# Two norm weights kept in the row ring of an expert-gathering decoder layer: twelve gather slots instead of fourteen

## The reference, cut to what matters

```
h  = x + mix
hn = rmsnorm(h, norm_ffn_w)
qry = hn @ w_q                      # 8 heads, two halves of 128
sv, si = top_k(scores, 16)          # per half
fv, fi = top_k(sums of pairs, 16)   # 16 experts per head, 128 picks per token
ue, ve = u[eidx], v[eidx]           # rows of 1024 floats, 4 KB each
act = gelu(einsum('thkd,td->thk', ue, hn))
y  = h + einsum('thk,thkd->td', gate * act, ve)
out = rmsnorm(y, norm_final_w)
```

## Time and profile before

| | us |
|---|---|
| median of three runs | 3558.62 |
| profiled execution, its time | 3555.45 |
| its span, first to last instruction | 3553.6 |
| PE busy | 2983.7 (84%) |
| POOL busy | 2434.8 (69%) |
| DVE busy | 2123.3 (60%) |
| ACT busy | 1522.3 (43%) |
| mean rate of the DMAs | 344 GB/s |

### The profile page before, as it was taken

One profiled execution on the slowest core, in us unless ns is written; L12 is line 12 of the kernel. 1 busy time (PEld: TensorE's weight loads), 2 busy tenths in 40 slices (PEclk: granted clock), 3 DMA queues, 4 the chain that ended last, 5 costly groups with the idle time before them and its releaser, 6 DMA issues.

```text
span 3553.6 us, 30435 instructions
## 1 busy us (share of the span) xinstructions
PE 2983.7 (84%) x8213; PEld 1385.9 (39%) x8213; DVE 2123.3 (60%) x4852; ACT 1522.3 (43%) x4094; POOL 2434.8 (69%) x2228
## 2 busy tenths in 40 slices
PE   6989699987898689878897889689968896589966
PEld 4844246443343244324432344234423442244221
DVE  2221655584658665866577657766676668454674
ACT  2021165334643474346533653365336633353333
POOL 1211276677777777777777777777777777576886
PEclk9999899999999999989998999899999999898999
DMA  5722499999999999999999999999999999898988
GB/s 189 264 83 70 151 405 354 358 341 385 385 388 375 369 394 379 388 370 402 370 395 362 405 372 380 370 407 374 392 359 407 381 388 359 317 358 308 347 315 346
DMA packets 346900, 1222.30 MB, mean 344 GB/s; under 512 B 39931, under 2 KB 51644, under 8 KB 345564
## 3 DMA queue, kind: packets, MB, share of 16 engines
q0 software_dynamic: 314272, 1140.57, 84.1%
q1 hardware_dynamic: 23596, 66.42, 5.1%
q10 hardware_dynamic: 8864, 13.37, 1.1%
HBM read 1195.56 MB, written 25.66 MB: 344 GB/s over the span
## 4 chain that ended last, share of the span: by engine, by line
PE 45%; POOL 21%; DMA 16%; DVE 8%; issue 7%; ACT 2%; SPq 0%; POOLq 0%; ACTq 0%; DVEq 0%
PE ps L1063 23%; DMA rows<-in_peer_v,idx 14%; POOL rows L452 11%; POOL rows L462 11%; PE ps L949 7%; PE ps L819 4%; PE ps L935 3%; PE ps L787 2%; DVE rows L1462 2%; PE ps L837 2%; DMA rows<-in_peer_u,idx 1%; DVE r L1353 1%; DVE r L1346 1%; PE ps L806 1%; DVE r L1347 1%
## 5 line engine op out<-in xcount | busy, mean ns | idle before, releaser
L1063 PE MATMUL ps<-rows,diag 128*128 128x512 f32 (+1 forms) x4224 | 2075.3, 624 | 468.9 <-DMA rows<-in_peer_v,idx 290.9
L1462 DVE CUSTOM_DVE_ANT_0 rows<-rows,hn_u 128x1024 f32<-128x1024 f32 x1056 | 1272.5, 1222 | 799.3 <-DMA rows<-in_peer_u,idx 794.8
L462 POOL DMA_INDIRECT rows<-in_peer_v,idx x1056 | 1200.5, 1137 | 429.7 <-issue 245.5
L1063 PEld LDWEIGHTS ps<-rows,diag 128*128 128x128 f32 (+1 forms) x4224 | 773.1, 195 | 1619.9 <-issue 1235.0
L452 POOL DMA_INDIRECT rows<-in_peer_u,idx x1056 | 1164.6, 1103 | 341.1 <-issue 321.7
L722 ACT ACTIVATE act_g<-act_g 128x1 f32<-128x1 f32 x1056 | 212.0, 201 | 1253.2 <-DVE act_g L1462 1245.9
L728 ACT ACTIVATE diag<-ident,act_g 128x128 f32<-128x128 f32 x1024 | 411.2, 402 | 344.1 <-PE ps L1063 317.1
L724 ACT ACTIVATE act_g<-act_g,gate 128x1 f32<-128x1 f32 x1056 | 311.0, 295 | 34.3
L949 PE MATMUL ps<-w_sc,r 128*128 128x512 f32 (+1 forms) x576 | 280.2, 594 | 0.0
L482 POOL DMA_DIRECT2D rows<-in_w_in x22 | 11.9, 539 | 228.9 <-PE ps L819 218.0
L722 ACT ACT_TABLE_LOAD x124 | 159.1, 1283 | 2.2
(11 more groups left out here) (270 smaller groups left out, 2114.1 us busy)
## 6 DMA issues: line engine op xcount, KB each, us to landing
rows<-in_w_in POOLq DMA_DIRECT2D x36, 512.0 KB, 3.9
rows<-in_peer_u,idx POOLq DMA_INDIRECT x1056, 6.6
rows<-in_peer_v,idx POOLq DMA_INDIRECT x1056, 6.6
r<-proj SPq DMA_DIRECT2D x8, 1344.0 KB, 10.5
rows<-in_w_in ACTq DMA_DIRECT2D x20, 512.0 KB, 6.6
w_sc<-in_w_q_t SPq DMA_DIRECT2D x8, 1024.0 KB, 7.4
proj<-rows POOLq DMA_DIRECT2D x22, 256.0 KB, 3.9
w_o<-in_w_in POOLq DMA_DIRECT2D x10, 512.0 KB, 6.6
```

The lines of the kernel that those rows point to most:

```text
L462: nc.gpsimd.indirect_dma_start(ring[:, slot, :], None, a["peer_v"], bass.IndirectOffsetOnAxis(ap=idx[g % 2][:, k:k + 1], axis=0), engine_s ...
L1063: last = nc.tensor.matmul(Y[j][0:m, :], diag[:, n % DIAGS, 0:m], ring[:, slot, 512 * j:512 * (j + 1)], start=(k == 0), stop=(k == steps_of ...
L1462: V.tensor_tensor_reduce(ring[:, slot, :], ring[:, slot, :], hn_u[:, :], 1.0, 0.0, ALU.mult, ALU.add, act_g[:, k:k + 1]).then_inc(S["dots" ...
```

## The change

Slots 12 and 13 leave the ring. They are named `w_ffn` and `w_fin`, and hold the two norm weights from the setup to the end. SP loads each once, in `load_front(0)`, after a wait for the last use of `keys` (`m_kept`). The loads per tile are gone, with SP's waits for `hn_taken` (except for the sampled tokens' own) and for `topk_done` ahead of them. The norm reads `w_ffn` instead of `hn`. The ring has 5 slots for `u` and 3 for `v` during tile 0, and 7 and 5 from tile 1 on. Slot 5 passes from `u` to `v`.

```diff
-U_EARLY, U_LATE = (0, 1, 2, 3, 4, 5), (8, 9)
-V_EARLY, V_LATE = (6, 7, 12, 13), (10, 11)
+U_EARLY, U_LATE = (0, 1, 2, 3, 4), (8, 9)
+V_EARLY, V_LATE = (5, 6, 7), (10, 11)
@@
-        w_fin = r2[:, D:2 * D]
+        w_ffn, w_fin = ring[:, 12, :], ring[:, 13, :]
@@ load_front(f)
                 if not is_sample(f):
                     sp.dma_start(pj, proj[f, :, 0:CHUNKS - 1, :]).then_inc(S["proj_in"], 16)
-                    if f:
-                        sp.wait_ge(S["hn_taken"], f)
-                    sp.dma_start(hn[:, :], a["norm_ffn"]).then_inc(S["w_ffn_in"], 16)
+                    if f == 0:
+                        sp.wait_ge(S["m_kept"], 2 * PH)
+                        sp.dma_start(w_ffn, a["norm_ffn"]).then_inc(S["w_ffn_in"], 16)
+                        sp.dma_start(w_fin, a["norm_final"]).then_inc(S["w_fin_in"], 16)
                     if f:
                         sp.wait_ge(S["kv_shifted"], f + 1)
                     sp.dma_start(k_t[:, 1, :], proj[f, :, CHUNKS - 1, :]).then_inc(S["proj_in"], 16)
@@ sample_caches(f)
                 sp.wait_ge(S["pv"], 2 * f + 2)
-                sp.dma_start(hn[0:NS, :], a["norm_ffn"][0:NS, :]).then_inc(S["w_ffn_in"], 16)
@@ SP, end of a period
-                    if f is not None:
-                        sp.wait_ge(S["topk_done"], f + 1)
-                        sp.dma_start(w_fin, a["norm_final"]).then_inc(S["w_fin_in"], 16)
@@ DVE, front(k, f), q == 87
-                    dve.wait_ge(S["w_ffn_in"], 16 * f + 16)
+                    dve.wait_ge(S["w_ffn_in"], 16)
-                    V.scalar_tensor_tensor(hn[0:n, :], hx[0:n, :], rstd[0:n, :], hn[0:n, :], ALU.mult, ALU.mult)\
+                    V.scalar_tensor_tensor(hn[0:n, :], hx[0:n, :], rstd[0:n, :], w_ffn[0:n, :], ALU.mult, ALU.mult)\
@@ DVE, finish(k, w), k == 4
-                    dve.wait_ge(S["w_fin_in"], 16 * min(w + 1, TILES))
+                    dve.wait_ge(S["w_fin_in"], 16)
```

## The result

The changed kernel takes 3602.14 us (median of 6 runs, 3595.63 to 3609.92) against 3565.03 us of the kernel before, run beside it (median of 6). The ratio is 1.0107 with a 95% interval of 1.0084 to 1.0130: 1.1% slower, or 37 us between the medians. The forecast was 3596 us and +37 us. That the sum came out does not say that its terms did, and three of them did not (tile 0's size, the setup and tile 7).

What follows compares the result with a forecast made beforehand. Six tiles were taken as bound by POOL's instruction stream and DVE's effect on it, not slots or bytes. Terms -1 + 2 + 22 + 8 + 6 = +37 us gave 3596 us, 1.0% slower, range 3553 to 3645.

Steps and rivals of the forecast that it cites:

- three signs that would have refuted it: Tiles 1 to 6 each 2 us shorter or more, tile 0 within 5 us of 414, or u gathers waiting for dots.
- The loads: Whole kernel: 7.5 MB less weight traffic, covered by POOL's stream, gives back 1 us, at most 18.
- The setup: Before the gathers: k_t issues near 170.0 us, lands 5.6 to 10.6 us later, PE stalls: +2 us.
- Tile 0: First tile with three v slots instead of four: longer rounds per pick, +22 us in all, from 3 to 44.
- Its first part: Tile 0's first 27 or so picks: three-slot rounds exceed POOL's 2.56 us pace, +8 us, from 3 to 12.
- its last: Tile 0 from 740 to 834 us: three-slot rounds and dots held back by DVE's top-k, +9 us, 0 to 24.
- the middle: Tile 0, 510 to 740 us: free while PE is full, except at three pauses of the added work, +5 us.
- Tiles 1 to 6: With five v slots POOL runs out one pick earlier at the last top-k steps: +8 us, 0 to 15.
- Tile 7: POOL is one pick less ahead when each of two clusters of PE stalls ends: +6 us, 0 to 15.
- The first rival: Bytes count after all: 18 us come back and the shorter ring costs little, 3543 us; chance 0.11.
- The second (all hidden): Landings shrink with the ring, lost picks are caught up; little but the setup's 2 us stays, 3561 us; chance 0.10.
- The third (lateness adds up, 3646 us): Landings don't shrink and tile 0, tiles 1 to 6, tile 7 and setup all cost more: +87 us; chance 0.19.

Runs made afterwards that it cites:

- second pair: Kernel before and changed kernel, both run and profiled again on one chip of 3565 us: ratios 0.9994 and 1.0099, profiled at 3586.97 and 3580.70 us.
- first pair: The original profiled executions of the kernel before and the changed kernel: 3555.45 us before, a span of 3599.1 us after.
- the even splits: Changed kernel with 4 u and 4 v slots in tile 0, 6 and 6 after, without or with the weights' loads moved later: 0.9987 each.
- e1_slots_only: Kernel before with the ring cut to 5 and 3 slots in tile 0, 7 and 5 after, all loads kept: 1.0046.
- e7_tile0_three: Kernel before with three v slots instead of four in tile 0 alone, full ring afterwards, loads kept: 1.0082.

## Why the prediction was right, and where it was not

The mechanism was right for tile 0: its loss is `v`'s slots, and neither bytes nor the sum of slots. The sum was +37 us, the medians give +37 and +34. That it fits so closely is partly luck: tile 0 was taken 5 to 13 us too low, the setup and tile 7 some 7 to 11 us too high, and 8 us for tiles 1 to 6 can be neither confirmed nor refused. Of the signs named, the landings near 6 us came, and the thirty first `v` gathers are 3.1 us apart, though only 14 of them show a wait for PE and not nearly each. Tile 0 (449 us for 436), tile 4 (373 for 360 to 368), tile 7 (435 for 445) and the first transposes (174.56 for 176 or later) were off. None of the three signs that would have refuted it came in this profile. In the second pair tiles 1 to 6 did fall by 5 us each, but there the longest execution of the one stands beside the shortest of the other. Term by term:

- **The loads** (-1, ends 0 and -18). Right as far as it was tested: the loads alone gave 3 us beside the full ring, with 0.5% excluded, on a chip of 3735 us. Beside the short ring they may be worth more: on the chip of 3565 us POOL's waits in tiles 1 to 6 are 13 us less without them (17.8 against 30.9), 7 of the 13 in the 16 `v` gathers that follow the first `u` gather of each tile (10.2 against 3.0 us), and the times differ by 9 us. But neither is clear of noise, and on the other chips the waits don't show it (61 and 67 us). That the loads stretch landings just there is not shown: the median over the `v` rows of the first 16 picks of these tiles is 8.1 us with loads and 7.8 without beside the short ring, and 9.8 and 7.8 in two executions of the kernel before.
- **The setup** (+2). Wrong, it is nothing. The step said that `k_t`'s issue would move to 170.0 us, and that it lands 5.6 us after that or later. The first was exact, and PE didn't wait:

```profile
170.00 0.43 SPq L361 DMA_DIRECT2D k_t<-proj  x1
```

```profile
174.56 0.60 PE L858 MATMUL ps<-ident,r 128*128 128x128 f32 x4
```

  The load landed 4.2 us after its issue, 0.3 us ahead of that use:

```profile
DMA to landing us min/median/max: 4.2/4.2/4.2
```

  The landings of the earlier trace rows were taken in traffic: at 151.5 us right behind 1.9 MB of other loads (the DMAs moved 377 GB/s from 150 to 162 us), and later among the gathers. From 169 to 176 us they moved 236 GB/s.
- **Tile 0** (+22, ends 3 and 44). The largest term and the right place, mis-sized: +35 us in the first pair of profiles, +27 in the second, +28 with three `v` slots alone. Its first part was +8 and is +10.5 and +6.6, its last +9 and +12 and +6. The part that failed is the middle, the sentence that "a slot fewer costs nothing while PE is full", at +5. It is +12.5 in the first pair and +13.7 in the second. PE's waits for `v` rows between picks 30 and 96, before and then after:

```profile
PE ps L1063 <- DMA rows<-in_peer_v,idx: 2.3, 6, 0.6
```

```profile
PE ps L1060 <- DMA rows<-in_peer_v,idx: 10.6, 11, 1.9
```

  Not three short meetings were added: PE waited eleven times instead of six, and longer. These waits make 8 of the 12.5 us (7 of the 13.7 in the second pair). In the rest PE is busy, 230.5 instead of 225.8 us: with a slot fewer POOL is less far ahead, and more of PE's work falls between the same two picks of POOL. What stalls PE is seen in its order. In the changed kernel:

```profile
544.48 1.88 PE L1060 MATMUL ps<-rows,diag 128*128 128x512 f32 x4
546.54 1.96 PE L1060 MATMUL ps<-rows,diag 128*128 128x512 f32 x4 [0.18 <-DMA rows<-in_peer_v,idx]
548.33 3.62 PE L834 MATMUL ps<-rows 128*128 128x256 f32 x16
551.78 1.05 PE L901 MATMUL ps<-r 128*128 128x128 f32 x8
552.68 3.60 PE L1060 MATMUL ps<-rows,diag 128*128 128x512 f32 x8
```

  The added work comes after every second pick, so PE takes two rows in a row and then none for 4.2 us or more. Over such a pair the ring must hold two rows that have landed while the third is under way. Three slots do this just so, and a late landing stalls PE. A mean busy share of 99% hid that. The reading is from PE's order and its waits; no kernel was run with the added work spread otherwise.
- **Tiles 1 to 6** (+8). Right in kind by the waits: 5.0 us became 17.3 in the first pair (78.2 us in 203 gaps, less 0.3 each) and 3.8 became 17.8 in the second. In time it can't be shown. The six tiles took 2178 and 2205 us in two executions of the kernel before, and 2189 and 2175 in two of the changed one. POOL's busy time in them scatters by more than the term:

```profile
839.00:3044.00 2205.00, 1842.06 (x4736) 812.49 (x4734) 1464.67 (x3295) 1074.57 (x2880) 1733.75 (x1537) 0.97 0.99 378
```

```profile
866.00:3040.00 2174.00, 1830.93 (x4729) 806.57 (x4729) 1463.29 (x3291) 1075.68 (x2877) 1689.11 (x1536) 0.97 0.99 380
```

  The first is the kernel before, 1733.8 us for 1537 POOL instructions, the second the changed one, 1689.1 us. The same gathers are 45 us shorter in all, in the pair of the longest and the shortest execution. In the first pair they are as good as equal, 1705.4 and 1703.6 us, and the kernel before alone differs by 28 us between its two profiles. Part may be that a POOL which waits for a slot doesn't stand behind DVE meanwhile; that was not tested apart.
- **Tile 7** (+6). Not seen: -3 us in the first pair, +1 in the second, although POOL waits 4 to 6 us more in it. Its gathers took 8 and 5 us less (309.4 and 301.4 us of POOL's busy time, 308.3 and 303.2), about what the waits added; whether the one causes the other was not tested. The waits grew as forecast; what failed is the step that adds them to the tile's time.

So the 45.5 us of the first pair are 4 before the first gather (scatter: the kernel before itself has it at 420.5 and 423.6 us), 35 in tile 0, 10 in tiles 1 to 6 (less than their scatter of 27), -3 in tile 7 and -1 behind it. Of the 34 to 37 us between medians, 27 to 35 are tile 0.

The first rival (bytes come back) fell by the kernel without loads. The second (all hidden) had half of a point: landings do shrink with the ring, from 6.6 to 5.9 us, but only 0.7 of the 1.3 us that a round would need to stay at 2.56 x 3. The third (lateness adds up, 3646 us) was right in that the middle of tile 0 gives nothing back.

What stays open is the other kind of chip. There the kernel before takes 3735 us, tiles 1 to 6 take 380 to 393 us whatever the kernel, the DMAs move 354 to 359 GB/s in them instead of 377 to 382, and the changed kernel's loss is 0.27% with tile 0's 27 us in full. In tiles 1 to 6 it took 2313 us, where kernels with all loads took 2330 to 2337. The saved loads alone don't explain this: the even splits, which save the same loads, took 2323 and 2334. And of two kernels that keep all loads on one chip, the one with the smaller ring throughout lost 17 us (`e1_slots_only`) and the one with the smaller ring in tile 0 alone 30 us (`e7_tile0_three`). Here are tiles 1 to 6 of these two, in this order:

```profile
872.00:3202.00 2330.00, 1874.65 (x4728) 821.30 (x4726) 1458.81 (x3290) 1070.42 (x2874) 1749.80 (x1536) 0.95 0.96 357
```

```profile
873.00:3206.00 2333.00, 1886.25 (x4729) 836.49 (x4729) 1454.50 (x3291) 1061.86 (x2877) 1757.06 (x1537) 0.94 0.96 357
```

The granted clock goes with it. Over whole executions its mean was 0.944 to 0.948 in the four kernels on these chips that have five `v` slots from tile 1 on, and 0.935 to 0.940 in the four that have six and in the kernel before; on the chips of 3565 us it was 0.957 to 0.960 in all kernels. A PE that is granted more may give part of the loss back on such a chip. This was not tested apart, and the cause is not settled.

## What to carry to other kernels

Price a slot by its round: issue to landing, plus the consumer's use, plus the way back, over the number of slots, against the pace of the issuing engine. As long as the round is the shorter one and the consumer takes its rows evenly, a slot is nearly free; once the round is the longer one, it costs the difference on every pick. Where the consumer takes rows in bursts, a mean busy share doesn't answer the question: look at how many rows it wants at once. Here the slot cost time that can be shown in one tile of nine. And before a ring is cut, split what is left by need: on the chip of 3737 us the same twelve slots as 4 and 4 instead of 5 and 3 cost nothing.

## What the runs showed of the hardware

A longer queue of gathers bought pace from three to four `v` slots and hardly any from four to five. At three, four and five `v` slots the median landing was 5.9, 6.6 (7.2 in a second execution) and 9.1 us, and from 440 to 500 us the DMAs moved 347 to 362, 409 and 409 GB/s. Rate times landing is what is in flight: 350 GB/s x 5.9 us is four gathers of 524 kB, 409 x 6.6 is five and 409 x 9.1 is seven. So a landing time taken in a full stream tells how many are in flight, not how long one needs.

A gather's issue on POOL takes 0.94 us, and beside two-input DVE operations 2.0 and 2.8 us, ending 0.8 us after them. In tiles 1 to 6 of the kernel before, POOL's 1537 instructions took 1705.4 us in one execution and 1733.8 in another. And the same binary differs by 4.8% from chip to chip (3565 and 3735 us), with a mean granted clock of 0.959 and 0.936, while DVE's dot takes 1.22 us on both.
